# Combining the expert rows of a two-layer mixture-of-experts kernel through DRAM instead of by matmul, and loading small tables earlier

## The reference, cut to what matters

```python
for l in range(2):
    h = rms_norm(x, attn_norm[l]); proj = h @ w_in[l]
    ...                                    # mixer -> y
    x = x + y @ w_out[l]
    x = x + hier_moe(rms_norm(x, ffn_norm[l]), ...)
x = second_block(x, ...)

# hier_moe: 32 experts, each token goes to 2 of them
h = silu(xi @ w1[e]) * (xi @ w3[e])        # 1024 -> 256
y = (h @ w2[e]) * rw[:, None]              # 256 -> 1024
out[row_tok] += y                          # a token's two rows are summed
```

## Time and profile before

| | us |
|---|---|
| median of 3 runs (range) | 1114.85 (1111.74 to 1114.96) |
| the profiled execution's own time | 1114.71 |
| its span in the trace | 1112.5 |
| PE, DVE, ACT, POOL busy | 1059.2, 405.4, 267.5, 101.9 |
| weight loads of PE, which overlap it | 540.3 |
| pair loops, first and second layer | 175 to 418, 592 to 835 |

### The profile page before, as it was taken

The page is one execution under the profiler, slowest core; times in us unless marked ns, Lnnn a source line. Parts: engine busy times, 40 slices in busy tenths (PEclk is TensorE's granted clock), DMA queues, the critical chain, the costliest instruction groups (busy, mean ns, idle before and its releaser), DMA issues.

```text
span 1112.5 us, 12936 instructions
## 1 busy us (share of the span) xinstructions
PE 1059.2 (95%) x4589; PEld 540.3 (49%) x4589; DVE 405.4 (36%) x985; ACT 267.5 (24%) x509; POOL 101.9 (9%) x148
## 2 busy tenths in 40 slices
PE   7999989999999996999989999999999999999998
PEld 4676654333333334676654333333334844555443
DVE  2263334433443431263334433443431222333220
ACT  3425321111111113225321111111112005554200
POOL 1320121000000001120121000000000200000000
PEclk9999999999999998999999999999999999999899
DMA  8528208999999998028208999999979537822000
GB/s 302 186 76 303 76 38 298 412 413 412 410 411 413 413 386 254 1 76 303 76 38 306 411 412 413 411 411 412 413 284 386 198 36 205 307 76 76 1 0 38
DMA packets 95596, 280.79 MB, mean 252 GB/s; under 512 B 16136, under 2 KB 29878, under 8 KB 87232
## 3 DMA queue, kind: packets, MB, share of 16 engines
q1 hardware_dynamic: 90192, 273.27, 64.6%
q0 software_dynamic: 5360, 6.94, 1.8%
HBM read 288.03 MB, written 4.72 MB: 263 GB/s over the span
## 4 chain that ended last, share of the span: by engine, by line
PE 70%; SPq 19%; DMA 4%; issue 2%; DVE 2%; ACT 2%; DVEq 0%; ACTq 0%
PE bank L1440 12%; SPq L575 12%; PE bank L911 10%; PE bank L1020 8%; PE bank L943 5%; PE bank L1214 5%; PE bank L1034 5%; PE bank L864 4%; SPq L581 3%; DMA ring<-in_w 3%; PE bank L1570 3%; SPq L622 3%; PE bank L1586 2%; PE bank L1458 2%; PE bank L853 2%
## 5 line engine op out<-in xcount | busy, mean ns | idle before, releaser
L911 PE MATMUL bank<-ring,arena 128*64 128x512 f32 x1024 | 229.8, 596 | 8.9 <-DMA ring<-in_w 8.8
L911 PEld LDWEIGHTS bank<-ring,arena 128*64 128x64 f32 x1024 | 73.9, 137 | 140.2 <-issue 126.5
L1440 PE MATMUL bank<-ring,xfT 128*128 128x512 f32 x320 | 141.5, 596 | 0.0
L943 PE MATMUL bank<-ring,arena 128*64 128x512 f32 x512 | 116.9, 599 | 0.0
L1020 PE MATMUL bank<-ring,xfT 128*128 128x384 f32 (+2 forms) x256 | 99.2, 543 | 2.9 <-DMA ring<-in_w_in 2.9
L864 PE MATMUL bank<-arena 128*128 128x512 bf16 x384 | 93.3, 379 | 0.0
L1440 PEld LDWEIGHTS bank<-ring,xfT 128*128 128x128 f32 x320 | 59.3, 190 | 69.3 <-issue 68.3
L1932 DVE TENSOR_TENSOR arena<-bank,arena 128x512 f32<-128x512 f32 x60 | 41.5, 692 | 119.3 <-ACT arena L1608 119.3
L1608 ACT ACTIVATE arena<-bank 128x512 bf16<-128x512 f32 (+1 forms) x64 | 38.2, 597 | 190.1 <-PE bank L943 190.1
L1020 PEld LDWEIGHTS bank<-ring,xfT 128*128 128x128 f32 x256 | 49.6, 198 | 44.6 <-issue 30.4
L1601 ACT ACTIVATE arena<-bank,arena 128x256 f32<-128x256 f32 x32 | 15.2, 475 | 218.1 <-PE bank L911 218.1
(11 more groups left out here) (374 smaller groups left out, 1121.5 us busy)
## 6 DMA issues: line engine op xcount, KB each, us to landing
ring<-in_w SPq DMA_DIRECT2D x256, 512.0 KB
ring<-in_w SPq DMA_DIRECT2D x64, 1024.0 KB
ring<-in_w_in SPq DMA_DIRECT2D x14, 2048.0 KB
ring<-in_w_in SPq DMA_DIRECT2D x8, 1536.0 KB
ring<-in_w_out SPq DMA_DIRECT2D x6, 2048.0 KB
ring<-in_w_in SPq DMA_DIRECT2D x2, 1696.0 KB
x_store<-x POOLq DMA_DIRECT2D x4, 512.0 KB, 3.0
ring<-in_w_up_moba SPq DMA_DIRECT2D x1, 2048.0 KB
```

The costliest lines, as they stand in the source:

```text
L911: ins = pe.matmul(bank[5][CELL * e:CELL * (e + 1), :], xg[:, par, 4 * h + k, at:at + CELL], view[:, e, :, k, :], start=(h == 0 and k == 0) ...
L943: ins = pe.matmul(bank[5 + n][CELL * e:CELL * (e + 1), :], turned[:, par, c, CELL * e:CELL * (e + 1)], down_view(s)[:, e, c, n * HALF:(n + ...
L1440: ins = pe.matmul(dst[:, :], xfT[:, k, t * P:(t + 1) * P], w[:, k, :], start=(k == 0), stop=(k == KD - 1))
```

## The change

- **Combining.** The rows of pairs 0 to 12 are not combined by PE. ACT copies both halves in float32 to `out_rows` (two buffers, one for each parity), POOL scatters them with one indirect DMA a pair into `y_store` in DRAM, a token's first choice at its number and its second 256 further, lanes without a row to row 512 or out of bounds. The scatter of a pair is issued three fetches later, behind a wait for its rows. ACT waits, before it writes `out_rows` again, for the scatter two pairs back. Pairs 13, 14 and 15 go by PE: `add_rows`, four float32 matmuls a pair, with `zero_acc` in pair 13. The three bf16 parts and all DVE work on them are gone.
- **Zero and read back.** In each layer SP fills the first 512 rows of `y_store` with zeros (2 MB, behind the router loads). Behind the last pair's weights it waits for the 13 scatters and reads the 512 rows back into `xf` and `xfT` (two loads of 1 MB). DVE adds them to `x` in four additions of 128 x 1024, behind the last pair's work and ahead of the four additions from the banks.
- **Store rows.** PE makes one more small table (L1407), DVE three small steps for `store_at`.
- **Gather.** Where a pair is not added by PE, bank 3 is free, and the second half of the next pair's rows is turned there straight behind the first half.
- **Small tables.** In the second layer `mixer_loads` come behind units 2 and 3 instead of behind all six, the other four units behind them. PE takes `rs` and `b2t0` ahead of `small` and `gate_w`, in both layers.
- **Start.** Unit 2 of the first layer is loaded in two halves, the first ahead of the second tile of `x`, and PE turns the second tile behind the first four matmuls. ACT loads its table with a small copy while it waits.
- The overflow count is made two pairs earlier.

```diff
+SCATTERED = PAIRS - 3
...
+            for half in range(2):
+                c0, c1 = UNIT_COLS[2]
+                sp.dma_start(unit_view(2, c1 - c0)[:, 4 * half:4 * half + 4, :], ...)\
+                  .then_inc(loaded_half if half == 0 else landed[2], 16)
+                if half == 0:
+                    sp.dma_start(x[:, 1, :], io["x"][0, P:2 * P, :]).then_inc(loaded_x[1], 16)
...
+                        if l and s == UNIT_ORDER[2]:
+                            sp.wait_ge(x_ready, PER * l)
+                            mixer_loads(l)
...
-                    if l:
-                        sp.wait_ge(x_ready, PER * l)
-                        mixer_loads(l)
                     router_loads(l)
+                    if l == 0:
+                        sp.wait_ge(loaded_consts, 16)
+                    else:
+                        sp.wait_ge(read_back, 32 * l)
+                    sp.dma_start(y_store[0:2 * SEQ, :].rearrange("(p r) (c n) -> p (r c) n", p=P, n=SEQ),
+                                 const["zeros"].unsqueeze(1).broadcast_to([P, 16, SEQ])).then_inc(y_zeroed, 16)
...
+                for a in range(2):
+                    sp.wait_ge(scattered[a], 16 * SCATTERS[a] * (l + 1))
+                for choice in range(2):
+                    sp.dma_start(y_back[choice], y_store[choice * SEQ:(choice + 1) * SEQ, :]
+                                 .rearrange("(t p) d -> p t d", p=P)).then_inc(read_back, 16)
...
                     fetch(pair, rows_at, rows_landed[pair % 2])
+                    if pair == 3:
+                        pool.wait_ge(y_zeroed, 16 * (l + 1))
+                        pool.wait_ge(store_known, l + 1)
+                    if pair >= 3:
+                        pool.wait_ge(main["y_ready"], 2 * (l * PAIRS + pair - 3) + 4)
+                        scatter(pair - 3)
...
-                combine(1 - par, 0, None if ahead else free[UP_HI[par]])
+                if add:
+                    add_rows(1 - par, 0, None if ahead else free[UP_HI[par]])
...
-                combine(1 - par, 1)
+                if add:
+                    add_rows(1 - par, 1)
...
+                dst = open_bank("rs")
+                pe.wait_ge(rstd_ready, 4 * l + 2)
+                done(spread_rstd(dst), "rs")
+                token_unit(3, "b2t0", 0, release=2)
                 pe.wait_ge(loaded_mixer, MIXER_LOADS * (l + 1))
...
+                if gone is not None:
+                    act.wait_ge(scattered[par], gone)
...
-                    act.activation(y_rest[:, n, :] if last else y_parts[:, par, 0, n, :], bank[5 + n][:, :], ACT.Copy)\
+                    act.activation(out_rows[:, par, n * HALF:(n + 1) * HALF], bank[5 + n][:, :], ACT.Copy)\
...
-                    dve.tensor_tensor(y_rest[:, n, :], bank[5 + n][:, :], y_parts[:, par, 0, n, :], ALU.subtract)\
-                    link(dve.tensor_copy(y_parts[:, par, 1, n, :], y_rest[:, n, :]))
...
+                dve.wait_ge(read_back, 32 * (l + 1))
+                for choice in range(2):
+                    for t in range(NT):
+                        step(dve.tensor_tensor(x[:, t, :], x[:, t, :], y_back[choice][:, t, :], ALU.add))
```

More of the change, by code:

```diff
@@ L891, in close_banks, with expert_pair @@
                             ins.then_inc(acc_done, 2 if t == 0 else 1)
-            def expert_pair(par, q, S, land, free, lands, fetched, rows, more=True):
+            def expert_pair(par, q, S, land, free, lands, fetched, rows, more=True, add=False, open_acc=False):
                 ahead = par == 0 or more
@@ L967, in _, with turn @@
             pe.wait_ge(loaded_first, 48)
-            def turn(m):
-                for t in range(NT):
+            def turn(m, tiles=range(NT)):
+                for t in tiles:
                     if m == 0:
@@ L1946, in gain_half, with expert_pair @@
                    .then_inc(S["xg_ready"], 1)
[L1948 removed]
+            def expert_pair(par, q, S, links, more=True, by_hot=False):
                 link = Chain(dve, S["vec"], links)
[L1950 to L1951 removed]
+                now, after = tables[:, par, :, :], tables[:, 1 - par, :, :]
+                if by_hot:
+                    link.note(dve.tensor_scalar(hot[:, par, :], tokens, now[:, 0, 0:1], None, ALU.is_equal))
+                link(dve.tensor_copy(after[:, :, 0:PAIRS - 1], now[:, :, 1:PAIRS]))
                 dve.wait_ge(S["silu_ready"], q + 1)
```

195 lines of the change are left out of this document (104 added, 91 removed).

## The result

The changed kernel takes 1135.85 us (median of 4 runs, 1130.84 to 1139.22), the kernel before, on the same chip, 1113.3 (1109.01 to 1114.96). The ratio is 1.0209, 95% interval 1.0186 to 1.0231: slower by 22.6 us, where 10.8 were forecast (1125.6, range 1110 to 1135). The profiled execution took 1137.98 us, its span is 1135.8, 23.4 more than before.

What follows compares the result with a forecast made beforehand. It took the pair loops to be bound by the DMA engines: -2.2 (start) + 11.1 (first layer's end) - 9.1 (tables) + 11.1 (second layer's end) = +10.9 us, giving 1125.6 us, range 1110 to 1135.

Steps and rivals of the forecast that it cites:

- The lag of some engines: End of the pair loops: rows in the first lanes load a few DMA engines more, so engines end some 10 us apart.
- 0.63 us a transfer: Pair loops: each row fetch or scatter costs the latest DMA engines 0.63 us, from 10 us/16.
- The tables: Second layer's start: loading small tables early lets rs and b2t0 fill the 6.15 us wait, -9.1 us.
- PE's tail: End of each loop: PE adds the last pairs in float32, +1.0 in the last pair and +0.5 in pair 14.
- even bytes: Rival for the pair loops: bytes spread evenly over the engines, stream 4.1 us late, total +2.9, 1117.6 us; chance 0.22.
- free writes: Rival for the pair loops: writes cost the reads nothing, stream not late, total -5.3, 1109.4 us; chance 0.14.
- an unfilled hole: Rival at the second layer's tables: units or tables land late, 3 instead of 9.1 us comes back, 1131.7 us; chance 0.11.
- the rival's 36 us: Clock rival: PE idles more in the loop, its clock falls, ten pairs lose 36 us, about 1160 us; chance 0.06.
- 13 x 0.63 = 8.1 us: Pair loops: 13 scatters a layer on the engines already late make each layer's weight stream 8.1 us later.
- The bound of 12: Upper end for the stream's delay in a layer, about 12 us, if a write costs half more than a read.
- the start, -2.2: Kernel's start: with unit 2 in halves PE begins sooner and ends at 24.1 against 26.3, bounds 0 and -3.5.
- the tail, d + 3.0: End of each layer's loop: DVE ends last, x ready d + 3.0 us later for a stream d late, 11.1 us.

Runs made afterwards that it cites:

- a1: The changed kernel without its 26 scatters, so x lacks the rows of 13 pairs a layer: 1114.72 us, 1.0029 of the kernel before.
- a2: The changed kernel with each expert's rows spread over the lanes, same bytes and instructions: 1117.47 us, 1.0049 of the kernel before.
- b1: The kernel before with each expert's rows spread over the lanes: 1105.7 us, 0.9946 of the kernel before.
- b3: The kernel before with each row fetch of both loops issued a second time, into a place nothing reads: 1140.64 us, 1.0264 of the kernel before.
- a4: The changed kernel with small tables and gate_w ahead of rs and b2t0 again in the first layer only: 1132.31 us, 1.0184 of the kernel before.
- a8: The changed kernel with the old start: unit 2 in one load, second tile of x ahead, both tiles turned first: 1138.02 us, 1.0229 of before.
- after: The changed kernel itself, with the whole change, against the kernel before: 1135.85 us, ratio 1.0209.

## Why the prediction was off

**What was right.** The loops were bound by the DMA engines and taking matmuls from PE gave nothing: without the scatter and its bytes (a1) the streams are as long as before. The lag of some engines and its cause, rows in the first lanes, stood in the prediction and held (a2, b1), and so did its size, 0.63 us a transfer, in the landings up to 14 us. The tables gave 8.3 us in the trace for 9.1 forecast. PE's tail was +1.5 and +1.4 for +1.5 (7.6 less 6.5 in its sum is 1.1, not 1.0, which changes nothing). DVE ended last, behind the read back. In the first data-bound pairs a scatter costs 32.9/2 - 15.8 = 0.65 us, for 0.63. The rivals of even bytes, free writes and an unfilled hole are refuted. The clock did fall in the loop, but the rival's 36 us didn't come, since data set the pace.

**Step one that failed: the stream, "13 x 0.63 = 8.1 us".** It measured 12.9 and 10.1 us, 6.8 more than forecast over two layers. The price of the first scatters was right, its use for all thirteen wasn't: from 320 us on a pair of the first layer takes 17.1 instead of 16.4 us and the GB/s fall to 381. The sum took the lag of the late engines as something that adds up while the others go on at full rate. The earlier trace rows shows a level 412 with 16 fetches, where the lag ends at 11.5 to 12.4 us; nothing in it shows what comes from 14 on. There the early parts of the loads run dry, and each pair costs 0.65 us more than the sum has; why the late ones lose that too isn't shown. The bound of 12 that I kept (for a dearer write) happened to hold most of it, but for another reason: b3 shows the same drop with reads.

**Step two: the start, -2.2.** It measured +2.4 at the first head unit. The bound I wrote down, unit 3 landing at about 24 us, was wrong: its last part lands at 27.6, and in the trace of before at 27.9, just ahead of `b2` at 27.98. (The time differs from trace to trace: 26.5 in a4, 29.3 in a8.) Before, the small tables and `rs` (1.75 us) stood in that wait as cover. The change moved `b1` forward and the tables behind, so that PE idled 3.1 us and lost the higher clock for half of `b2`. The table at 294 GB/s says how much is moved in 25 us, not in which order it lands.

**Step three: the tail, d + 3.0.** By the end of the additions to `x`, which the term forecast, it measured d + 4.6 in the first layer and d + 4.3 in the second: about 1 us of it stands between DVE's two groups of additions, the rest has no single place. By the first product behind it, it is 3.0 and 4.2: in the first layer PE's turn began 1.3 us behind the last addition before, and begins directly behind it now.

Together 6.8 (streams) + 5.0 (start, 2.8 for -2.2) + 1.2 (tails) + 0.8 (tables) - 1.3 (last block) = 12.5 us, the difference between 23.4 and 10.9.

## What to carry to other kernels

Where a stream of weights fills the DMA engines, price a small transfer by the engine that gets most of it, not by its bytes; put sparse rows into lanes far apart, which costs nothing and gave 6 us of 1112 even without the change. A lag read from the end of a stream adds up only to a point, here 14 to 16 us between the first and the last landing of a load: read the sixteen landings, and how soon the first follows its issue, to see how near the early engines are to running dry. Before moving work forward, look at what it covers now: the small tables stood in a wait for a load in the first layer and in front of one in the second, and the same reordering lost 2 us in the one and gave 9 in the other.

## What the runs showed of the hardware

Indirect transfers with all rows out of bounds cost nothing that can be measured (26 of them, 3744 more packets, 1115.54 against 1114.72 us). A second fetch of the rows of a pair, 32 rows of 4 KB on average, cost 0.9 us in the packed lanes (29 us over 32 fetches) and 0.4 to 0.5 in spread ones (1.0068 - 0.9946 is 13.6 us, 1121.63 - 1105.7 is 15.9), where their bytes at 412 GB/s would be 0.3. A DMA share of 1.00 to 1.02 can go with 298 to 386 GB/s (after, 325 to 375 us): the share alone doesn't tell that the stream is at its full rate, the GB/s beside it does. The difference is in single packets: one of 4 KB mostly takes 0.16 us and one of 8 KB 0.31, but from 350 to 375 us 186 packets of after take longer than 0.17 and 0.33, up to 1.75, 33 us over the usual time in all, or 8% of the time of sixteen engines (in the same 25 us of the kernel before 15 packets, 0.2 us over the usual time).
